# Moving convolution taps, modulation copies and waits in a two-layer hybrid block on one core

## The reference

```python
# first block, mixer
h = rms_norm(x, mix_pre_g) * (1 + sc1) + sh1
q, k, v, f_logit, conv_val, conv_gate = split(h @ w_in)
attn = softmax(q k^T / 8 + cum[t] - cum[s], causal) @ v        # 8 heads of 64
u = conv_val * sigmoid(conv_gate)
u = silu(layer_norm(causal_depthwise_conv(u, conv_w, conv_b))) # 31 taps, 512 channels
x = x + g1 * rms_norm(concat(attn, u) @ w_o, mix_post_g)
x = x + g2 * rms_norm(swiglu(rms_norm(x) * (1 + sc2) + sh2), ffn_post_g)
# second block: Mamba-2 layer, then
k, v = split(modulate(x, kv_norm_g, kv_shift, kv_scale) @ kv_w) # 16 heads of 64
q, z = split(modulate(x, norm_g, shift, scale) @ in_w)
a = sigmoid(logits) * prod of sigmoid(-logits) over later keys
x = x + gate * ((a @ v * silu(z)) @ out_w)
out = rms_norm(x, final_g)
```

## Time and profile before

| | |
|---|---|
| three runs | 1438.09, 1435.17, 1441.22 us; median 1438.09 |
| the profiled execution | 1437.19 us |
| its span, first to last instruction | 1435.4 us |
| mean granted TensorE clock | 0.97 |
| PE busy | 1360.9 us (95%) |
| DVE busy | 823.6 us (57%) |
| ACT busy | 588.3 us (41%) |
| DMA queue of SP | 33% of the 16 engines' time |

### The profile page before, as it was taken

One profiled execution on the slowest core, in us unless ns is written; L12 is line 12 of the kernel. 1 busy time (PEld: TensorE's weight loads), 2 busy tenths in 40 slices (PEclk: granted clock), 3 DMA queues, 4 the chain that ended last, 5 costly groups with the idle time before them and its releaser, 6 DMA issues. The chain is left out here.

```text
span 1435.4 us, 19530 instructions
## 1 busy us (share of the span) xinstructions
PE 1360.9 (95%) x7904; PEld 1078.1 (75%) x7904; DVE 823.6 (57%) x965; ACT 588.3 (41%) x848; POOL 405.6 (28%) x191
## 2 busy tenths in 40 slices
PE   5999999889999999999999999988998999999996
PEld 3777867668888888887788876766776898777774
DVE  3789853476655544333757556677733822466544
ACT  4323656333222222112444456776522422455451
POOL 0000000039987887998100000000000050233310
PEclk9999999989999999999799999999999999999998
DMA  9433061215454455553222243333122432110121
GB/s 384 160 134 132 30 235 63 84 34 210 177 194 180 171 218 191 190 191 147 92 89 88 96 126 89 118 118 133 59 102 86 151 132 89 59 60 30 59 89 59
DMA packets 41350, 181.12 MB, mean 126 GB/s; under 512 B 3392, under 2 KB 20160, under 8 KB 21312
## 3 DMA queue, kind: packets, MB, share of 16 engines
q1 hardware_dynamic: 40128, 171.73, 33.2%
q10 hardware_dynamic: 1152, 8.39, 1.7%
HBM read 173.75 MB, written 6.36 MB: 125 GB/s over the span
## 5 line engine op out<-in xcount | busy, mean ns | idle before, releaser
L193 DVE TENSOR_TENSOR wlo<-raw,whi 128x2048 fp32r<-128x2048 f32 x95 | 260.8, 2745 | 183.1 <-ACT whi L189 180.6
L200 POOL TENSOR_TENSOR ada_raw<-ada_raw,cs 128x2048 f32<-128x2048 f32 x36 | 142.0, 3944 | 509.6 <-DVE h2lo L451 458.6
L271 PE MATMUL ps<-hhi,whi 128*128 128x512 f32 x640 | 252.0, 394 | 2.4 <-PEq L562 0.8
L271 PE MATMUL ps<-hhi,wlo 128*128 128x512 f32 x640 | 249.4, 390 | 0.0
L271 PE MATMUL ps<-hlo,whi 128*128 128x512 f32 x640 | 249.1, 389 | 0.0
L189 ACT ACTIVATE whi<-raw 128x2048 fp32r<-128x2048 f32 x95 | 181.5, 1911 | 143.6 <-PE ps L1309 91.3
L209 POOL TENSOR_TENSOR ada_raw<-ada_raw 128x1024 f32<-128x1024 f32 x72 | 169.4, 2353 | 5.6
L271 PEld LDWEIGHTS ps<-hhi,whi 128*128 128x128 f32 x640 | 120.2, 188 | 28.6 <-issue 2.4
L271 PEld LDWEIGHTS ps<-hhi,wlo 128*128 128x128 f32 x640 | 120.1, 188 | 25.7
L271 PEld LDWEIGHTS ps<-hlo,whi 128*128 128x128 f32 x640 | 120.3, 188 | 24.3
L2036 POOL TENSOR_TENSOR x<-x,rest 128x256 f32<-128x256 f32 (+3 forms) x32 | 49.0, 1532 | 163.7 <-DVE rest L2331 163.7
(11 more groups left out here) (373 smaller groups left out, 2806.4 us busy)
## 6 DMA issues: line engine op xcount, KB each, us to landing
raw<-panels SPq DMA_DIRECT2D x87, 1024.0 KB, 4.9
ada_raw<-ada SPq DMA_DIRECT2D x48, 1024.0 KB, 6.7
first<-ada SPq DMA_DIRECT2D x8, 1024.0 KB, 19.6
bc<-ac_rows SPq DMA_DIRECT2D x32, 256.0 KB, 3.7
raw<-panels ACTq DMA_DIRECT2D x8, 1024.0 KB, 5.1
x_kept<-x SPq DMA_DIRECT2D x2, 2048.0 KB, 9.6
x<-x_kept SPq DMA_DIRECT2D x2, 2048.0 KB, 8.2
x<-x_in SPq DMA_DIRECT2D x1, 2048.0 KB, 9.3
```

The costliest lines, as they stand in the source:

```text
L193: e.tensor_tensor(wlo[:, c % 2, :, :], raw[:, c % 2, :, :], whi[:, c % 2, :, :].bitcast(F32), ALU.subtract).then_inc(lo_split, 1)
L200: e.tensor_tensor(ada_raw[:, c % 2, :, :], ada_raw[:, c % 2, :, :], cs[:, which, :].unsqueeze(2).to_broadcast([P, KT, 256]), ALU.mult).the ...
L271: mm = e.matmul(ps[:, 2 * (qc % 2) + b, :], w[:, c % 2, 2 * k + b, :], src[part][:, k, :], **flags)
```

## The change

The arithmetic stays the same; instructions move.

1. Fewer taps stand in the last two panel steps and in unit 0, and more in units 11 to 14 (`DENSE_TAPS`, `UNIT_TAPS`). In units 11 and 12 ACT makes the copy of the second modulation slice right behind the exponentials, ahead of `normalise` and `take`. `read_mod(dve, 8, 20)` stands first in unit 15 of DVE's list. `w13` is issued behind `a19`.
2. `SUMS_AFTER`: in the post norms and in the final stage PE makes the sums of squares in groups behind banks 3, 5 and 7 and no longer behind each bank.
3. In the pre norms PE runs the four matmuls that need `hhi` alone first and waits for `hlo` only then.
4. The coefficients of `pre1` and `pre2` are formed earlier.
5. In the second attention the q panel is the eighth and the last v panel the ninth. `logits(0)` no longer waits for the ninth panel's copy; the first `project` does. The split of panel `c0 + 10` moves behind unit 0's sigmoids and scans, and ACT loads the sigmoid table early.

```diff
+        SUMS_AFTER = {3: (0, 1, 2), 5: (3, 4), 7: (5, 6)}
...
                 for j, b in enumerate(ORDER):
                     part(b).then_inc(N["bank_done"] if j < KT - 1 else panels_used, 1)
-                    if j == 2:
+                    if j == 3:
                         pe.wait_ge(*no("kept", 1))
-                        token_sums(pe, no, 0, 0, sq, ORDER[0])
-                    if j >= 2:
-                        token_sums(pe, no, 0, j - 1, sq, ORDER[0])
+                    for t in SUMS_AFTER.get(j, ()):
+                        token_sums(pe, no, 0, t, sq, ORDER[0])
...
                 for k in range(k0, k1):
-                    pe.wait_ge(*no("lo_ready", k + 1))
-                    for b in range(2):
-                        for n, (w, part) in enumerate(PASSES):
-                            mm = pe.matmul(ps[:, 2 * (qc % 2) + b, :], w[:, c % 2, 2 * k + b, :],
...
+                    for part, weights in ((0, (whi, wlo)), (1, (whi,))):
+                        pe.wait_ge(*no("lo_ready" if part else "hi_ready", k + 1))
+                        for b in range(2):
+                            for w in weights:
+                                mm = pe.matmul(ps[:, 2 * (qc % 2) + b, :], w[:, c % 2, 2 * k + b, :],
...
-                DENSE_TAPS = [11, 11, 11, 9, 5, 10, 2]
-                UNIT_TAPS = [5] * 11 + [2, 4, 4, 0, 0]
+                DENSE_TAPS = [11, 11, 11, 9, 5, 9, 0]
+                UNIT_TAPS = [1] + [5] * 10 + [4, 5, 6, 2, 0]
...
                         order = ["w4", "w5", "w6", "a10", "a11", "w7", "w8", "w9", "w10", "a12", "a13", "w11", "w12", "a14", "a15",
-                                 "w13", "a16", "a17", "a18", "a19", "a20", "a21", "w14", "w15", "w16", "w17"]
+                                 "a16", "a17", "a18", "a19", "w13", "a20", "a21", "w14", "w15", "w16", "w17"]
...
                                 ins.then_inc(A["exp"], 1)
+                            if n in (11, 12):
+                                ada_keep(act, ROWS_AT[n][1], MODB, 256)
                             if 1 <= n <= NU:
                                 normalise(n - 1)
...
-                            if n in ROWS_AT:
+                            if n in (13, 14):
                                 ada_keep(act, ROWS_AT[n][1], MODB, 256)
...
                         for n in range(NU + 3):
+                            if n == 15:
+                                read_mod(dve, 8, 20)
...
-                            if n == 15:
-                                read_mod(dve, 8, 20)
...
+                        pre1["coefs"](dve)
                         post1["dve"](dve)
-                        pre1["coefs"](dve)
                         pre1["dve"](dve)
...
             def place(j):
 
+                if j in (7, 8):
+                    return c0 + 15 - j
...
-                        if j == 8:
+                        if j == 7:
                             pre4["all_low"](pe)
-                        in_panel(pe, c0 + j, q0 + j, 0, (h2hi, h2lo) if j == 8 else (hhi, hlo), 4 <= j < 8)
+                        in_panel(pe, c0 + j, q0 + j, 0, (h2hi, h2lo) if j == 7 else (hhi, hlo), j in (4, 5, 6, 8))
...
                         if n == 0:
-                            pe.wait_ge(pair_free[0], (q0 + 8) // 2 + 2)
                             pe.wait_ge(pair_free[1], (q0 + 7) // 2 + 2)
...
+                            if mh == 0:
+                                pe.wait_ge(pair_free[0], (q0 + 8) // 2 + 2)
...
-                        split_hi(act, c0 + j + 2, 0)
+                        if j < 8:
+                            split_hi(act, c0 + j + 2, 0)
+                        if j == 7:
+                            act.activation(warm[:, 7:8], ones[:, 0:1], ACT.Sigmoid)
...
+                        if n == 0:
+                            split_hi(act, c0 + 10, 0)
```

More of the change, by code:

```diff
@@ L473, in on_pe @@
                 for k in range(k0, k1):
-                    pe.wait_ge(*no("lo_ready", k + 1))
-                    for b in range(2):
-                        for n, (w, part) in enumerate(PASSES):
-                            mm = pe.matmul(ps[:, 2 * (qc % 2) + b, :], w[:, c % 2, 2 * k + b, :],
-                                           (thi, tlo)[part][:, k, :], start=(k == 0 and n == 0),
-                                           stop=(k == KT - 1 and n == 2), skip_group_check=True)
+                    for part, weights in ((0, (whi, wlo)), (1, (whi,))):
[3 more added lines that the diff above has]
+                                mm = pe.matmul(ps[:, 2 * (qc % 2) + b, :], w[:, c % 2, 2 * k + b, :],
+                                               (thi, tlo)[part][:, k, :], start=(k == 0 and part == 0 and w is whi),
+                                               stop=(k == KT - 1 and part == 1), skip_group_check=True)
                 if k1 == KT:
@@ L2186, in _ @@
                         mm.then_inc(nsem["bank_done"] if j < KT - 1 else panels_used, 1)
-                        if j == 2:
-                            token_sums(pe, fin, 0, 0, fsq, ORDER[0])
-                        if j >= 3:
-                            token_sums(pe, fin, 0, j - 2, fsq, ORDER[0])
-                    for j in range(KT - 2, KT):
-                        token_sums(pe, fin, 0, j, fsq, ORDER[0])
+                        for t in SUMS_AFTER.get(j, ()):
+                            token_sums(pe, fin, 0, t, fsq, ORDER[0])
+                    token_sums(pe, fin, 0, KT - 1, fsq, ORDER[0])
                     spread(pe, fin, 0, ORDER[0])
@@ L2201, in _ @@
                         bank = ps[:, 2 * pair:2 * pair + 2, :]
-                        if 4 <= j < 8:
-                            r = j - 4
+                        if j in (4, 5, 6, 8):
+                            r = min(j - 4, 3)
                             act.activation(v2[:, :, r * 256:(r + 1) * 256],
@@ L2283, in _ @@
                                               ALU.subtract).then_inc(pair_free[pair], 1)
-                        elif j == 8:
+                        elif j == 7:
                             dve.wait_ge(B["qhi"], 1)
@@ L2288, in _ @@
                                                      op1=ALU.subtract).then_inc(pair_free[pair], 1)
-                        split_lo(dve, c0 + j + 2, 0)
+                        if j < 8:
+                            split_lo(dve, c0 + j + 2, 0)
                         if j < 2:
@@ L2333, in _ @@
                             scan.then_inc(B["rest"], 1)
+                        if n == 0:
+                            split_lo(dve, c0 + 10, 0)
                         if n >= STEPS and n % STEPS == 0 and n // STEPS <= HALVES:
```

2 lines of the change are left out of this document (1 added, 1 removed).

## The result

| | before | changed |
|---|---|---|
| four runs each, one chip | 1435.17 to 1441.22, median 1438.68 us | 1417.04 to 1419.63, median 1418.30 us |
| profiled execution | 1437.19 us | 1418.72 us |
| its span | 1435.4 us | 1416.9 us |
| ratio | | 0.986, 95% interval 0.9837 to 0.9883 |

The changed kernel is 20.4 us faster by the medians and 18.5 us faster in the two profiled executions; 1420 us was forecast.

The account below looks back on a forecast made before the run. PE was taken as the bound, busy 1360.9 of 1435.4 us. First attention 8.2, sums 3.7, pre norms 2.1 and second attention 4.0 sum to 18.0: 1437.2 - 18.0 = 1419.2, 1420 for the median, range 1413 to 1429.

Parts of the forecast that it names:

- Start of the first attention: Unit 2: PE's 2.40 us stop and half the 3.4 us low stretch behind it go; gain 4.1, bounds 2.4 and 4.7.
- Early copies: Unit 11: the 1.13 us copy stop goes but returns as a transfer wait; gain 0, bounds 0 and 1.1.
- `w13`: Unit 13: a16, issued ahead of `w13`, lands before PE comes; gain 1.1 us, bounds 0 and 1.15.
- Low stretch of unit 12: 195.2 to 202.3: behind 198.8 the loss is 1.7 us, half taken as gain, 0.9; bounds 0 and 1.7.
- The prediction's own sign of being wrong: Forecast wrong if PE stands for DVE's maxima in units 11 to 14, or the clock is low longer in the units.
- End: First attention from unit 15: of 3.9 us in stop and low stretch, 2.1 kept, 1.8 become ACT waits; bounds 0.5 and 3.9.
- Sums: Grouped sums gain 1.3 us in each of two post norms and 1.1 in the final stage; 3.7 together, bounds 2 and 3.9.
- Pre norms: PE starts earlier on `hhi`: 1.0 us, 0.8 ahead of second attention, 0.3 ahead of Mamba; together 2.1, bounds 1.0 and 4.
- Second attention: The 2.37 us stop ahead of the first logits and the low stretch's 1.6 go; gain 4.0, bounds 1.5 and 4.3.
- the clock gives more: Rival: low stretches elsewhere, above all ahead of pre-norm panels, shorten too; 6 us more, 1414; chance 0.10.

Follow-up runs that it names:

- slices are shifted: Changed kernel with the modulation slices one place earlier, slice 12 in unit 10 to slice 19 alone in unit 14: 1421.30 us, 0.9890.
- the slices alone: Kernel before with only the earlier modulation copies, `w13` behind `a19` and the earlier read in unit 15: 1434.15 us, 0.9973.
- the whole first attention: Kernel before with the tables of taps and the edits to slices, `w13` and the read together: 1429.78 against 1436.85 us, 0.9956.
- the order undone: Changed kernel with the pre-norm matmul order as before, all three products of a tile behind its rest: 1423.50 us.
- the repeat: Changed kernel run once more in a later job, beside the kernel before: 1422.26 against 1437.35 us, 0.9892.
- the norms alone: Kernel before with only the grouped sums, the pre-norm order of matmuls and the moved coefficients: 1433.46 us, 0.9979.

## Why the prediction was right, step by step

- **Start of the first attention, 4.1.** Measured 4.1 in all ten traces that have the taps' tables (where slices are shifted, up to unit 10). Unit 1's maximum came 3.4 us earlier, between the 2.7 and 4.7 counted. In the four traces without the tables the stop of 2.4 us has its low stretch behind it each time, and units 2 to 3 take the same 5.89 us. That no later unit would wait for DVE holds as well.
- **Early copies, 0.** Right: 3.4 without, 3.3 with.
- **`w13`, 1.1.** 1.5 with `w13` undone. The stop is 1.17; that the transfers ahead of it move a little too wasn't in the step.
- **Low stretch of unit 12, 0.9 by "I take half", bounds 0 and 1.7.** This is the term whose size was off, both ways. In the first trace units 11 to 14 gained 3.6 where 0.9 + 1.1 was forecast. From slice 15's rows (198.84 before, 194.00 now) to the logits of unit 15 the gain is 2.9: the stop of 1.15, and 1.7 for the low stretch, all of it and not half. The other 0.7 lies ahead of these rows and is in no term: slice 15 took 6.0 us to land where the forecast kept the 6.7 of before. In the two traces on the second chip with all edits of these units the gain was -0.6 and -2.7, and two kernels there without an edit in these units stood at -0.8 and -2.2. So in those traces, compared like with like, the gain of these units is about nothing. The medians can be asked too: the slices alone, 3.4 - 2.3 for the end, leave 1.1, and the whole first attention, 7.1 - 4.1 - 2.3, leaves 0.7, about what `w13` is worth. The bounds had neither the spread of the landings nor a doubling of the stretch to 14. The prediction's own sign of being wrong, a clock low for longer than before in the units, stands in the trace with the order undone: 14.5 us against 3.4 + 7.1 + 3.4 = 13.9 before.
- **End, 2.1.** 2.3, in every trace that has the read first and ACT's list as in the change. From the end of the last logits to the transposes of unit 15 it takes 7.3 us (212.68 to 220.01), where 7.5 was counted along ACT's list. The stops for DVE and ACT are 0.47 + 0.78 = 1.25; the forecast had 0.5 to 1.5, all for ACT.
- **Sums, 3.7.** 1.3 + 1.2 + 1.1 = 3.6. The price of a change-over, 0.36, taken from two distances, carried over to both post norms and the final stage.
- **Pre norms, 2.1.** The starts came earlier as foretold, the ends less so. From the spread to the panel's first matmul it took 4.75 us ahead of the feed-forward layer, 4.55 with the coefficients moved and the order old, and 3.76 in the changed kernel; ahead of the Mamba layer 4.73, 4.53 and 4.27. So the coefficients are 0.2 in each place, and the rest is the order's. At the panels' ends about 1.1 of the 2.1 is left by the means, near the lower bound of 1.0, and only 0.6 in the first pair of traces (0.3 - 1.0 + 1.3). That bound was put for a clock that rises at the same moment whatever the start; the clock there wasn't tested by itself.
- **Second attention, 4.0.** 3.5. 0.29 us stand for the v copy, which the forecast let the logits just cover; the low stretch is gone, but cost 1.3 to 1.4 and not the 1.6 of half its length.

The sum was 18.0. The profiled executions differ by 18.5 (1437.19 - 1418.72); the terms come to 4.1 + 3.6 + 2.3 + 3.6 + 0.6 + 3.5 = 17.7 for that pair, and 0.8 lie in stages that no edit touched. By the medians the same change was worth 20.4 in the first measurement and 15.1 in the repeat. The forecast lies between the two. That it came so near the first pair's 18.5 is luck in part: units 11 to 14 gave 1.6 more than forecast, with full clock throughout and a quick slice 15, and the pre norms gave 1.5 less. The rival "the clock gives more" had expected more from the clock ahead of the pre norms, where it didn't come.

The transfers: slice 14, issued with no other transfer in flight, took 4.8 us in the changed kernel. The estimate by the Trainium skill, "DMA: Bandwidth & Descriptors", section "Anatomy of one DMA", is 4.4 us for 1 MB. That section is about transfers that GpSimd issues, which the prediction didn't say, and SP issues these. Slice 15, issued 2.1 us behind slice 14, took 5.7 to 8.1 over the twelve traces that have it there, 6.0 in the changed kernel's first. So the sum comes near the first transfer of a pair and is 1.3 to 3.7 us short for the second, and mostly the longer stop of unit 12 is the second's.

## What to carry to other kernels

Price a stop of the bound engine and the clock stretch behind it as two things. A stop for another engine repeated to 0.1 us from trace to trace here, a stop for a transfer didn't (1.11 and 2.00 us for slice 15). The stretch behind the stops of 2.40 and 2.37 us came each of the nine times that one of them stood in a trace, at the same price; behind the stops of 1.13 and 2.16 us it was anything from nothing to 14 us at half speed, so there both ends belong in the range. Judge a change of a few us by medians taken side by side, and use the traces stage by stage, between landmarks, for the parts in which the clock behaves alike in all of them. Moving a slow read or a release ahead of a wait in a helper engine's list, without taking any work away, was worth 2.3 us in one place, and 1.2 in another by one trace.

## What was not expected of the hardware

- The same stop of PE for the same copy, 1.13 us, was followed by 14 us at 0.51 in one kernel and by none in another; the stop of 2.16 us ahead of the mean was followed by 3.4 us at 0.50 before, by 7 with the taps alone and with the second attention alone, and by none in the kernel with the norms alone:

```profile
225.32 1.08 PE L876 MATMUL ps<-cv,consts 128*32 128x128 f32 x32 [2.16 <-DVE mod L252]
```

```profile
225.00:230.00 5.00, 4.68 (x59) 1.00 0.02 3
```

What decides it isn't settled here.
- Of two 1 MB transfers issued 2.1 us apart in unit 11 the second took 6.0 and 6.7 us in the two traces of the first measurement, 6.2 to 6.5 in the four of the third chip and 5.7 to 8.1 in the eight of the second. What spreads them there wasn't tested.
- A stage that no edit touched, the Mamba layer up to its last spread, was 1.0 us shorter in the changed kernel's first trace: the low stretch near 1000 us lasted 7 us before and 4 after. In the kernels with the taps alone and with the second attention alone, which have no edit there either, it lasted 4 as well, so this too changes from execution to execution.
